# Banded attention in one fused two-block kernel: every score product over all 128 rows, with both token halves in one accumulation

## The reference, cut to what matters

```
q, k = rope(q, pos), rope(k, pos)                  # 256 tokens, 64 wide
s = (q @ k.T) * 64 ** -0.5                          # 256 x 256, kept where -128 <= query - key <= 128
p = exp(s - m) / (sum(exp(s - m)) + exp(sink - m))  # m = max over the keys and the sink
o = p @ v
```

## Time and profile before

| | |
|---|---|
| median of 3 runs | 1487.23 us (1483.44, 1487.23, 1487.77) |
| the profiled execution | 1484.44 us, its span 1483.1 us |
| PE busy | 1423.4 us, 96% of the span |
| DVE busy | 932.0 us, 63% |
| ACT busy | 724.0 us, 49% |
| POOL busy | 231.7 us, 16% |
| windowed attention | about 701 to 842 us of the span; its 16 window heads 728.4 to 799 |

### The profile page before, as it was taken

The page is one execution under the profiler, slowest core; times in us unless marked ns, Lnnn a source line. Parts: engine busy times, 40 slices in busy tenths (PEclk is TensorE's granted clock), DMA queues, the critical chain, the costliest instruction groups (busy, mean ns, idle before and its releaser), DMA issues.

```text
span 1483.1 us, 23163 instructions
## 1 busy us (share of the span) xinstructions
PE 1423.4 (96%) x9623; PEld 1264.5 (85%) x9623; DVE 932.0 (63%) x1506; ACT 724.0 (49%) x1054; POOL 231.7 (16%) x190
## 2 busy tenths in 40 slices
PE   6899999999999999998999999999999998799998
PEld 5887799999898899996776799999689987699997
DVE  5744476667784866676456165656465787665655
ACT  4434345555452445553655355444457775554453
POOL 2571200000000000002622500000133333100000
PEclk9999999999998999999999999999999999999999
DMA  8332145655463456452412355555344434355551
GB/s 302 140 129 114 58 171 176 236 181 190 174 231 128 163 179 227 173 197 96 160 58 86 114 199 185 213 192 178 137 172 146 143 118 157 137 187 180 205 198 57
DMA packets 36554, 240.40 MB, mean 162 GB/s; under 512 B 3873, under 2 KB 6241, under 8 KB 8930
## 3 DMA queue, kind: packets, MB, share of 16 engines
q1 hardware_dynamic: 36450, 238.92, 44.3%
HBM read 236.27 MB, written 2.64 MB: 161 GB/s over the span
## 4 chain that ended last, share of the span: by engine, by line
PE 87%; DVE 6%; ACT 2%; POOL 2%; issue 2%; DMA 0%; SPq 0%; ACTq 0%; DVEq 0%
PE ps L359 24%; PE ps L326 16%; PE ps L328 16%; PE ps L327 16%; PE ps L481 2%; PE ps L488 2%; POOL wlo L276 2%; PE ps L810 1%; PE ps L1615 1%; ACT whi L268 1%; PE ps L469 1%; DVE gb L2078 1%; PE ps L978 1%; DVE wlo L283 1%; PE ps L708 1%
## 5 line engine op out<-in xcount | busy, mean ns | idle before, releaser
L326 PE MATMUL ps<-XS,whi 128*128 128x256 f32 x2088 | 599.2, 287 | 17.8 <-POOL wlo L276 4.9
L327 PE MATMUL ps<-XS,whi 128*128 128x256 f32 x2088 | 594.8, 285 | 0.0
L328 PE MATMUL ps<-XS,wlo 128*128 128x256 f32 x2088 | 594.6, 285 | 0.0
L283 DVE TENSOR_TENSOR wlo<-raw,whi 128x2048 fp32r<-128x2048 f32 x163 | 372.5, 2287 | 126.7 <-ACT whi L268 126.4
L268 ACT ACTIVATE whi<-raw 128x2048 fp32r<-128x2048 f32 x204 | 388.8, 1907 | 117.8 <-PE ps L359 79.3
L326 PEld LDWEIGHTS ps<-XS,whi 128*128 128x128 f32 x2088 | 405.0, 194 | 24.1 <-issue 12.8
L327 PEld LDWEIGHTS ps<-XS,whi 128*128 128x128 f32 x2088 | 404.9, 194 | 1.8 <-issue 0.2
L328 PEld LDWEIGHTS ps<-XS,wlo 128*128 128x128 f32 x2088 | 404.6, 194 | 0.0
L359 PE MATMUL ps<-whi,MS 128*128 128x512 f32 x1024 | 292.5, 392 | 5.9 <-POOL wlo L276 3.5
L276 POOL TENSOR_TENSOR wlo<-raw,whi 128x512 fp32r<-128x512 f32 x162 | 214.8, 1362 | 502.3 <-ACT whi L268 429.4
L359 PEld LDWEIGHTS ps<-whi,MS 128*128 128x128 f32 x1024 | 189.3, 188 | 46.2 <-POOL wlo L276 4.3
(11 more groups left out here) (282 smaller groups left out, 1360.8 us busy)
## 6 DMA issues: line engine op xcount, KB each, us to landing
raw<-in_up SPq DMA_DIRECT2D x88, 1024.0 KB, 4.8
raw<-in_down SPq DMA_DIRECT2D x44, 1024.0 KB, 4.8
raw<-in_hg_t SPq DMA_DIRECT2D x16, 1024.0 KB, 4.8
raw<-in_od_t SPq DMA_DIRECT2D x8, 1024.0 KB, 4.9
raw<-in_ev_a SPq DMA_DIRECT2D x7, 1024.0 KB, 8.0
raw<-in_wa_o SPq DMA_DIRECT2D x6, 1024.0 KB, 4.8
raw<-in_hg_o SPq DMA_DIRECT2D x6, 1024.0 KB, 4.7
raw<-in_ev_o SPq DMA_DIRECT2D x4, 1024.0 KB, 7.0
```

The source lines that it names most:

```text
L283: ve.tensor_tensor(lo[:, 0:w], r[:, 0:w], hi[:, 0:w].bitcast(F32), ALU.subtract).then_inc(w_lo_v)
L326: pe.matmul(d, hi[:, c], S[:, k, 0:256], start=(k == 0), stop=False)
L327: pe.matmul(d, hi[:, c], S[:, k, 256:512], start=False, stop=False)
L328: last = pe.matmul(d, lo[:, c], S[:, k, 0:256], start=False, stop=(k == 7))
```

## The change

`KL` becomes two chunks of `MS` and takes the form of `KD`: for each half `r` the 64 rows of that half hold the keys' low part and the other 64 rows hold zeros. The second product therefore runs over all 128 rows; what the zeros meet adds nothing. The zeros are written by two new DVE memsets in `split_dve(0)`. The four products of both token halves come first and the two masks last, and the six matmuls form one accumulation: `start` on the first products of the first half alone, `stop` on the last mask alone. The number of matmuls stays at six for a head.

```diff
-        KL = MS[:, 10, :].rearrange("p (j t) -> p j t", j=2)
+        KL = MS[:, 10:12, :].rearrange("p c (r t) -> p c r t", r=2)
...
         def window_score(o, i):
             c, r, h = whead(i)
-            q = slice(64 * r, 64 * r + 64)
             pe.wait_ge(r_qs.sem, 2 + c // 2)
             for tt in range(2):
                 t = slice(128 * tt, 128 * tt + 128)
-                pe.matmul(o[:, 256 * tt:256 * tt + 256], QS[:, c, r, t], KD[:, c // 4, r, :], start=True, stop=False)
-                pe.matmul(o[:, 256 * tt:256 * tt + 256], QS[q, c, r, t], KL[q, c // 4, :], start=False, stop=False)
+                pe.matmul(o[:, 256 * tt:256 * tt + 256], QS[:, c, r, t], KD[:, c // 4, r, :], start=(tt == 0), stop=False)
+                pe.matmul(o[:, 256 * tt:256 * tt + 256], QS[:, c, r, t], KL[:, c // 4, r, :], start=False, stop=False)
+            for tt in range(2):
                 d = o[:, 128:256] if tt == 0 else o[:, 256:384]
-                last = pe.matmul(d, identb, cmb if tt == 0 else cmb2, start=False, stop=True)
+                last = pe.matmul(d, identb, cmb if tt == 0 else cmb2, start=False, stop=(tt == 1))
             return last
...
                 if i == 0:
                     src = KR[head_rows(r), :].rearrange("p (j t) -> p j t", j=2)
-                    ins = ve.tensor_tensor(KL[head_rows(r)], src, KD[head_rows(r), :, r, :].bitcast(F32), ALU.subtract)
+                    ve.memset(KL[head_rows(1 - r), :, r, :].bitcast(F32), 0.0)
+                    ins = ve.tensor_tensor(KL[head_rows(r), :, r, :], src, KD[head_rows(r), :, r, :].bitcast(F32), ALU.subtract)
```

## The result

| | before | after |
|---|---|---|
| median of 20 runs | 1485.47 us (1481.1 to 1489.67) | 1478.78 us (1475.81 to 1485.98) |
| ratio of the two | | 0.9964, 95% interval 0.9949 to 0.9978 |
| the profiled execution | 1484.44 us, span 1483.1 | 1477.91 us, span 1476.6 |

The changed kernel is 0.36% faster by the ratio, which on 1485.5 is 5.3 us. The means of the 20 runs, 1485.4 and 1480.0, lie 5.4 apart; the medians lie 6.7 apart. One kernel's runs differ by more than that (8.6 us before, 10.2 after), so the stage itself has to show where the gain comes from.

What follows compares the result with a forecast made beforehand. TensorE was taken to bound the kernel, losing time at each change of row number in the scores. Gains of 0.4 + 1.3 + 1.7 + 1.9 = 5.3 us, from the mean of 1485.7, gave 1480.4; range 1475.5 to 1487.0.

Steps and rivals of the forecast that it cites:

- heads 0 to 3: First stretch of the windowed attention: 0.4 us gained of 2.6, with memsets making the first scores 0.57 late.
- heads 8 to 12: Windowed attention, heads 8 to 10 and 11 to 12: 1.7 us gained of 3.2, limited by DVE and POOL's pieces.
- One head's scores: TensorE, first score product to transposes: 0.70 us behind value products, 0.60 behind `project`, saving 0.64 a head from 1.34.
- the prediction's signs: What would show it in the trace, including all 32 second products with 128 rows starting 0.12 after the first.
- Heads 4 to 7: Second stretch of the windowed attention: 1.3 us gained of 2.6, the rest lost waiting for DVE before head 4's transposes.
- 0.3 us better: Before head 9's transposes: the sum if L851 alone, not the small L846 too, waits for POOL's fourth piece.
- Heads 13 to 15: Last stretch of the windowed attention: 1.9 us gained of 1.9, no rope or POOL, DVE just keeping up.
- Waits don't eat it: Rival for the windowed heads: up to 9.6 us gained, 1476.1, if POOL and DVE waits fall otherwise; chance 0.10.
- A new wait takes most: Rival for the windowed heads: only 3 us gained, 1482.7, bounds 0.5 to 3.5; chance 0.24.
- three mechanisms: Mask drains once a head (0.45 instead of 0.64 saved), first stretch gives nothing, DVE's lag shows in the last stretch.
- The clock: Rival: TensorE's clock also falls before head 4's transposes; two stretches of 10.2 give +3.5, 1489.2; chance 0.07, including one stretch.
- Full-row products don't overlap: Rival for the scores: four products at 0.31, no gain, memsets' 0.57 remains, 1486.3; chance 0.03.

Runs made afterwards that it cites:

- e1: Kernel before with only the change's order and accumulation flags, low product still over 64 rows, no zeros; 1485.21 us against 1484.25, ratio 1.0004.
- e3: Changed kernel with full rows and zeros, but the old order and a start and stop for each token half; 1480.83 us against 1484.25, ratio 0.9970.
- e4: Changed kernel with the two memsets moved ahead of DVE's first rope; 1481.26 us against 1484.25 before, ratio 0.9983.
- e5: Changed kernel with the ropes of passes 1 and 5, and the split behind each, one pass later; 1477.55 us against 1486.74 before, ratio 0.9939.
- e8: Kernel before with the ropes of passes 1 and 5 one pass later; one run, 1483.02 us.
- e10: Changed kernel with early memsets and the later ropes of passes 1 and 5 together; 1478.94 us against 1487.02 before, ratio 0.9953.
- e6: Changed kernel with ACT's high part of the next weight tile ahead of the queries' split in pass 10; 1479.40 us against 1486.74 before, ratio 0.9955.
- e7: Changed kernel with e4, e5 and e6 together, and ACT's high part of pass -1 left to pass 3; 1481.60 us against 1486.74 before, ratio 0.9954.
- e9: Changed kernel with early zeros, later ropes, and ACT's next high part ahead of the split in passes 3, 7, 10; 1479.47 us against 1486.85 before, ratio 0.9941.
- e2: Changed kernel with 64-row low products and no zeros: both 128-row products, both 64-row ones, masks last; 1482.21 us against 1484.25 before, ratio 0.9996.

## Why the prediction came out right

**The size.** Forecast 5.3 us of gain and 1480.4 us of time; measured 5.3 by the ratio, 5.35 by the stage, and a median of 1478.78 (mean 1480.0). The stage bears the forecast out. That the ratio does so to 0.1 us is luck, since the same two kernels measured again gave 9.1. The sum is also better than its terms: 0.3 too much for heads 0 to 3 and 0.4 too little for heads 8 to 12 nearly cancel.

- *One head's scores, 0.70 behind value products and 0.60 behind `project`.* Measured 0.71 and 0.60. All 32 second products have 128 rows. They start 0.12 behind the first in the second token half always, in the first half only behind `project` (0.20 at head 0, after its wait). Behind value products or masks it is 0.22, which the sum had and the prediction's signs left out, and behind the rotation matmul of 512 columns 0.52. The masks' change of type costs nothing, as the earlier trace rows let me assume. By e1 and e3 the cause is the rows: four changes at about 0.2 each before, none now.
- *Heads 0 to 3, 0.4 us.* Measured 0.11, the term with the largest error for its size. The memsets took 0.48 each as forecast, but I had DVE's low parts 0.93 later and they were 1.28. DVE's timeline:

```profile
721.62 0.48 DVE L1665 MEMSET MS<- 64x512 f32 x1 [0.16 <-issue]
722.12 0.68 DVE L1666 TENSOR_TENSOR MS<-ar,MS 64x512 fp32r<-64x512 f32 x1
722.86 0.48 DVE L1665 MEMSET MS<- 64x512 f32 x1
723.36 0.69 DVE L1666 TENSOR_TENSOR MS<-ar,MS 64x512 fp32r<-64x512 f32 x1
724.08 1.39 DVE L1669 TENSOR_TENSOR MS<-ar,MS 64x512 fp32r<-64x512 f32 x2
```

  The first memset starts 0.16 late with nothing but "issue" ahead of it, and neither overlaps its neighbours: the first takes 722.12 - 721.46 = 0.66 out of DVE's time, the second 723.36 - 722.80 = 0.56, and the 0.08 by which the first L1665 of the kernel before (L1666 now) began ahead of the rope's end is lost as well. So the scores began 1.01 late, not 0.57, and POOL's tile was stretched by 0.57, not 0.3. e4 took the memsets away from there and gained 0.55. That more was not lost is because TensorE waits for DVE at head 0's transposes anyway (2.16).
- *Heads 4 to 7, 1.3 us.* Measured 1.26. The wait of 0.32 became 1.59, as forecast: over 1.5. e5 moved the rope out of the way and got 1.69 back there.
- *Heads 8 to 12, 1.7 us.* Measured 2.12. (By the prediction's own rounded terms L851 would end at 782.22, not 782.15, which is 1.6.) The wait before head 9's transposes was forecast at about 0.8 and is 0.88, and POOL stretches DVE as said. What is better is that the small operation between did not wait. DVE's timeline:

```profile
773.47 0.68 DVE L828 TENSOR_SCALAR ar<-ar 128x2 f32<-128x2 f32 x1
774.07 0.15 DVE L846 TENSOR_TENSOR ar<-ar 128x2 f32<-128x2 f32 x1
...
774.45 1.32 DVE L851 TENSOR_SCALAR ar<-ar 128x256 f32<-128x256 f32 x2
```

  L828 ends with POOL's third piece, L846 slips in in 0.15, and L851 (two of them, 0.62 alone) takes the fourth piece in 1.32. That is the "0.3 us better" which the prediction gave for this case. It isn't that L846 is too short to be held: it began 0.01 us ahead of POOL's fourth piece (774.08). In e8 the same operation began 0.07 behind the start of a piece and took 1.24. Timelines of DVE and POOL there:

```profile
762.64 1.24 DVE L846 TENSOR_TENSOR ar<-ar 128x2 f32<-128x2 f32 x1
...
762.57 1.28 POOL L276 TENSOR_TENSOR wlo<-raw,whi 128x512 fp32r<-128x512 f32 x1
```

  In "SBUF — State Buffer", Who interferes with whom, the Trainium skill has a `tensor_tensor` with both inputs in SBUF contend with GpSimd's reads; e8's row agrees with it.
- *Heads 13 to 15, 1.9 us.* Measured 1.85; DVE just keeps up.

**The rivals.** *Waits don't eat it* (9.6): 3.7 us of new waits for L851 say no, and what takes them away is known from e4, e5 and e10. *A new wait takes most* (3): the masks don't drain, which was its main condition. The first stretch did give almost nothing (0.11), so one of its three mechanisms came true, and heads 8 to 12 paid for it. *The clock:* no new lower-clock stretch in the stage; the old one was there, of 3.4 us in place of 6.8 in this profile. Elsewhere it differs from run to run. *Full-row products don't overlap:* they do. The rule of the Trainium skill ("TensorE: Matmul & The Clock Gate", Part 3, The mechanism), by which a weight load overlaps matmuls in flight only when its row group differs, does not hold here as it is worded: matmuls whose loads all have 128 rows start 0.12 us apart, and it is the change of the rows that costs. The same section names the background weight buffer as a second case in which a load is pulled ahead, and no run here shows whether that is what happens.

**The experiments that fell short** are alike: I counted what an earlier or later tile of POOL no longer delays, and not what it then meets. e5 gave 2.18 of 3.2, e6 0.30 of 0.9, e7 1.04 of 5, e9 0.3 of 4. e10, which moves DVE's own work, and POOL's tiles only with it, came out as expected in the stage.

**What stays open.** Why the two measurements of the changed kernel differ by 3.7 us with stages equal to 0.01 us. The stretches at the lower clock summed to 51.8 to 65.3 us in the 13 profiles, most of them in places that no edit touches, and the spans don't simply follow these sums. Within the 20 runs of the changed kernel the time does follow the mean granted clock: the three longest (1485.64 to 1485.98 us) had 0.976, the three shortest (1475.81 to 1476.57) 0.983. Most other series follow it less, and the 19 runs of the kernel before beside e5 to e8 hardly at all (the longest, 1489.85, had 0.980, the shortest, 1480.83, 0.979). So the clock accounts for much of the spread in the first and not for all of it, and not for the 3.7 us.

## What to carry to other kernels

Read the start of one matmul to the start of the next: where neighbours have different numbers of rows, some 0.2 us goes at each change, and padding the smaller operand with zeros to 128 rows cost less than either order of the small ones that was tried (e1, e2). Then follow the engine that feeds TensorE's next step: here half of 10.2 us saved turned into waits for DVE, at the two ropes and where GpSimd's pieces meet DVE's SBUF-only operations. To win those, move the DVE work itself (rope, memsets) away from the wait, which took 2.6 us more off the stage in e10, and put a GpSimd tile nowhere before you have looked up what DVE does in its new place; and judge edits of 2 us in a stage by the stage, not by a run of 1480. Where you leave a stretch out because of the clock, look whether the lower clock begins ahead of it, and who came last there: in e8 that hid half of the gain.

## What was not expected of the hardware

- A memset of 64x512 between other DVE operations takes 0.48 us and costs 0.64 (1.28 for two), since it neither starts at once nor overlaps.
- A DVE operation of two numbers a row takes 0.23 us alone and up to 1.33 beside a GpSimd piece of 1.24; a pair of L851 takes 0.62 alone, 1.32 beside one piece, and 2.33 to 2.38 beside a row of them. An operation that begins just ahead of a piece isn't held: L846 took 0.15 when it began 0.01 ahead and 1.24 when it began 0.07 behind (e8).
- The stage's length, without the piece at the lower clock, was the same to 0.01 us in two profiles of one kernel, while the whole kernel's time spreads over some 9 to 10 us.
- At the lower clock one head's scores of the kernel before took 2.16 us (e8), at the full clock 1.34.
